# Packed wave tables, and the first weight tiles and gates brought forward, in a hybrid recurrence and Fourier block on one core

## The chip, the cores and the metric

The kernel runs on one core of one Trainium2 chip. Its metric is the device time of one execution in microseconds (us), of which several runs are given. TensorE is called PE here, VectorE DVE, ScalarE ACT, GpSimd POOL and SyncE SP; each works through its own instructions in order and waits on semaphores for the others.

## What is computed

A token block (2048 x 1024, float32) is normalised and projected by W_in. Half of the projection feeds a bidirectional gated recurrence with 8 heads, the other half a Fourier mix; both are gated and projected together by W_out, added to the input and normalised again. The parts that the change touches are the Fourier mix and the output product:

```python
def fourier_mix(u, w_four, b_four):
    ug = u.reshape(b_, length, FOURIER_GROUPS, FOURIER_GROUP_DIM)       # 4 groups of 256 channels
    spec = jnp.fft.fftn(ug, axes=(1, 3), norm="ortho").real
    y = jnp.einsum("blgc,gcd->blgd", spec, w_four).reshape(b_, length, FOURIER_WIDTH)
    return y + b_four
...
    y_a = o.reshape(h.shape[:-1] + (HGRN_WIDTH,)) * jax.nn.silu(gate_a)
    y_f = fourier_mix(u_f, w_four, b_four) * jax.nn.silu(gate_f)
    out = jnp.concatenate([y_a, y_f], axis=-1) @ w_out                  # W_out is 2048 x 1024
```

## The kernel before

Every float32 product is made of three passes over a high and a low part (`mm3`, L58 to L63): high by high, low by high, high by low. So each operand is split first: ACT copies it to the high part, DVE subtracts that from the raw values for the low part. All stages run in one program: `front` (norm, projections of the context, folded token sums), `heads` (projections and recurrence, up to about 1625 us of the trace) and `tail` (from there on), which the change touches.

`tail` has two halves. **The Fourier half** walks over four groups of 256 channels (`for n in range(FG)`). A group has, on PE: `middle(n)` (two small matmuls, L2673), `channels(n)` (eight steps f that fill the banks `ps_p`), then `waves(n, 0)` and `waves(n, 1)`, the transforms over time with the wave tables `tab_hi`, `tab_lo` for two blocks of 128 channels (m = 2n + c counts them), each with four arrays in the order 0, 2, 1, 3 and a few narrow matmuls at the end (L2724 to L2727, `ps_top`). ACT splits the high part of p (`split_p_high`), DVE the low part (`split_p_low`); PE may run only three steps of `channels` ahead of the low splits, since four banks hold p. After the transforms ACT copies the sine arrays out (`copy_sine`) and DVE joins them with the cosine arrays to y (`combine`, odd arrays by way of `mixed`); SP stores y to memory. DVE also folds the next group's input (`fold_again`, `split_fold_low`). All engines take these steps in an order written out by hand.

**The output half** multiplies the 16 row tiles of 128 tokens by W_out. W_out stands as 16 tiles of 128 x 1024 in on-chip memory, split too (`split_w_high` on ACT, `split_w_low` on DVE); tiles 8 to 15 belong to the Fourier rows, 0 to 7 to the heads. `W_ORDER` is the order of the splits, and j counts in it. A weight tile takes the place of something that is no longer read, so POOL waits before each load (`load_w`, L2045). PE starts with `f_part(0)`, `f_part(1)`, `f_part(2)` over six of eight Fourier tiles (`F_FIRST = 6`), which need the weights j = 0 to 5 and the gated, split rows `f_raw`, loaded from y in memory together with their gates `f_gate` (`load_f` on SP). Then come `turn_heads(0)` (transposes of the scaled head outputs), the remaining tiles, and `a_part`.

In the kernel before, all eight Fourier weight tiles are loaded and split in the last group (n = 3, `last`): the four wave tables take 64 KB, of which each 16 KB place holds only 4 KB of high and 4 KB of low part, and the folded input takes the rest.

## Time and profile before

| | |
|---|---|
| time, median of 3 runs (lowest to highest) | 2125.49 us (2124.35 to 2126.05) |
| the profiled execution | 2122.28 us |
| its span | 2120.3 us |
| mean granted clock of PE | 0.991 |
| PE busy | 2052.2 us (97%) |
| DVE busy | 1542.4 us (73%) |
| ACT busy | 537.6 us (25%) |
| chain that ended last | PE 88%, DVE 7%, issue, ACT, DMA and SP's queue 1% each |

The span runs from the first to the last instruction; the 2.0 us between it and the execution's time lie around it. "Busy" is a share of the whole span and tells little of one stage. The granted clock is a share of TensorE's full 2.4 GHz; 0.50 is 1.2 GHz. A row of a timeline gives start, duration, engine and line, the operation as out<-in, and in brackets the idle time before it and who ended it.

### The profile page before, as it was taken

Reading aid. Unit: us, or ns where it says so; the run is one execution under the profiler, and the core shown is the slowest. Engines: PE = TensorE matmul, PEld = TensorE weight load, DVE = VectorE, ACT = ScalarE, POOL = GpSimd, SP = SyncE. Lnnn points to the kernel's source line nnn. Section 1 sums busy time; section 2 is a strip of 40 time slices with the busy share of each in tenths; the row PEclk is TensorE's granted clock in tenths of the full one; section 3 lists DMA queues with packets and bytes.
Section 4 is the critical chain, followed back from the end, with each engine's and each line's share of the span. In section 5 each row is a group of like instructions: output and inputs, shape, how many; then the busy total and the mean of one; then the engine's idle time right before and its main releaser. Section 6 shows DMA issues by size and latency. Waiting matters only on the chain.

```text
span 2120.3 us, 51238 instructions
## 1 busy us (share of the span) xinstructions
PE 2052.2 (97%) x21168; PEld 1759.9 (83%) x21168; DVE 1542.4 (73%) x3318; ACT 537.6 (25%) x968; POOL 75.1 (4%) x109
## 2 busy tenths in 40 slices
PE   5899999999999999999999999999998989999997
PEld 2799998898888888888888888888887877888886
DVE  4865864143887878878887878799998986665664
ACT  3721134211122222212212221222213443222221
POOL 0001102000000000000000000000000010000000
PEclk9999999999999999999999999999999999999999
DMA  9534554323423324343333334243434377456461
GB/s 378 195 115 152 165 175 137 124 88 96 134 88 116 123 89 144 96 125 104 119 116 107 115 98 141 86 143 96 129 111 152 110 274 230 166 164 200 157 204 59
DMA packets 242542, 298.03 MB, mean 141 GB/s; under 512 B 15187, under 2 KB 172527, under 8 KB 240268
## 3 DMA queue, kind: packets, MB, share of 16 engines
q1 hardware_dynamic: 157868, 177.33, 26.5%
q10 hardware_dynamic: 74096, 81.18, 11.5%
q0 software_dynamic: 10352, 36.25, 5.4%
q8 instruction: 173, 2.83, 0.6%
q14 instruction: 53, 0.43, 0.1%
HBM read 197.11 MB, written 97.59 MB: 139 GB/s over the span
## 4 chain that ended last, share of the span: by engine, by line
PE 88%; DVE 7%; issue 1%; ACT 1%; DMA 1%; SPq 1%; ACTq 0%; DVEq 0%; POOL 0%
PE all_bank L61 19%; PE all_bank L63 19%; PE all_bank L62 19%; PE all_bank L1494 5%; PE all_bank L1500 5%; PE all_bank L1497 5%; PE all_bank L1572 3%; PE all_bank L1348 2%; PE all_bank L1528 2%; PE all_bank L1515 2%; PE all_bank L1565 1%; PE all_bank L71 1%; PE all_bank L1554 1%; PE all_bank L1347 1%; DVE hidden_h_lo L483 1%
## 5 line engine op out<-in xcount | busy, mean ns | idle before, releaser
L61 PE MATMUL all_bank<-hidden_h_hi,head_hi 128*128 128x512 f32 x718 | 288.1, 401 | 0.0
L63 PE MATMUL all_bank<-hidden_h_hi,head_lo 128*128 128x512 f32 x718 | 280.3, 390 | 0.0
L62 PE MATMUL all_bank<-hidden_h_lo,head_hi 128*128 128x512 f32 x718 | 279.9, 390 | 0.0
L1610 ACT ACTIVATE head_projected<-all_bank 128x512 f32<-128x512 f32 x148 | 88.6, 598 | 728.2 <-PE all_bank L63 460.9
L1494 PE MATMUL all_bank<-hidden_h_hi,head_hi 128*128 128x512 f32 x466 | 192.0, 412 | 0.6
L1708 DVE RECIPROCAL head_inverse<-head_gate 128x448 f32<-128x448 f32 x64 | 185.1, 2926 | 0.0
L1500 PE MATMUL all_bank<-hidden_h_hi,head_lo 128*128 128x512 f32 x466 | 182.2, 391 | 0.0
L1497 PE MATMUL all_bank<-hidden_h_lo,head_hi 128*128 128x512 f32 x466 | 181.9, 390 | 0.0
L63 PEld LDWEIGHTS all_bank<-hidden_h_hi,head_lo 128*128 128x128 f32 x718 | 134.8, 188 | 28.7
L61 PEld LDWEIGHTS all_bank<-hidden_h_hi,head_hi 128*128 128x128 f32 x718 | 134.9, 188 | 27.7
L62 PEld LDWEIGHTS all_bank<-hidden_h_lo,head_hi 128*128 128x128 f32 x718 | 135.1, 188 | 25.4
L61 PE MATMUL all_bank<-front_hi,hidden_h_hi 128*128 128x256 f32 x512 | 143.3, 280 | 0.0
L62 PE MATMUL all_bank<-front_lo,hidden_h_hi 128*128 128x256 f32 x512 | 142.3, 278 | 0.0
L63 PE MATMUL all_bank<-front_hi,hidden_h_lo 128*128 128x256 f32 x512 | 142.3, 278 | 0.0
L1375 DVE SCALAR_TENSOR_TENSOR head_state<-head_state,head_total,all_bank 128x128 f32<-128x128 f32 x256 | 71.8, 343 | 82.0 <-issue 65.3
L1748 DVE TENSOR_TENSOR head_query_planes<-head_query_planes,head_total 128x256 f32<-128x256 f32 x128 | 54.0, 422 | 71.9 <-PE all_bank L1515 35.4
L61 PE MATMUL all_bank<-tail_w_hi,tail_f_hi 128*128 128x512 f32 x256 | 101.0, 394 | 4.7 <-DVE tail_f_lo L2274 4.7
L1500 PEld LDWEIGHTS all_bank<-hidden_h_hi,head_lo 128*128 128x128 f32 x466 | 87.4, 188 | 19.4
L1494 PEld LDWEIGHTS all_bank<-hidden_h_hi,head_hi 128*128 128x128 f32 x466 | 87.5, 188 | 19.0 <-DVE head_lo L1652 1.9
L61 PE MATMUL all_bank<-tail_w_hi,tail_a_hi 128*128 128x512 f32 x256 | 101.5, 396 | 1.1 <-DVE tail_a_lo L2307 1.1
L62 PE MATMUL all_bank<-tail_w_lo,tail_f_hi 128*128 128x512 f32 x256 | 100.6, 393 | 0.0
L63 PE MATMUL all_bank<-tail_w_hi,tail_f_lo 128*128 128x512 f32 x256 | 100.5, 392 | 0.0
(327 smaller groups left out, 4778.3 us busy)
## 6 DMA issues: line engine op xcount, KB each, us to landing
head_raw<-in_w_in POOLq DMA_DIRECT2D x37, 512.0 KB, 5.0
head_value<-value_rows SPq DMA_DIRECT2D x64, 256.0 KB, 4.7
head_query<-piece_query SPq DMA_DIRECT2D x64, 256.0 KB, 5.6
head_out<-head_o ACTq DMA_DIRECT2D x64, 256.0 KB, 2.6
tail_o<-head_out SPq DMA_DIRECT2D x32, 512.0 KB, 6.5
front_raw<-in_w_in SPq DMA_DIRECT2D x19, 512.0 KB, 5.0
front_stage<-in_x SPq DMA_DIRECT2D x16, 512.0 KB, 6.6
front_w_mod<-in_w_ada SPq DMA_DIRECT2D x8, 1024.0 KB, 13.7
```

What stands on the lines that cost most here:

```text
L61: nc.tensor.matmul(out, st_hi, mv_hi, start=start, stop=False)
L62: nc.tensor.matmul(out, st_hi, mv_lo, start=False, stop=False)
L63: return nc.tensor.matmul(out, st_lo, mv_hi, start=False, stop=stop)
L1348: done = nc.tensor.matmul(ps[d][2][:, t, :], tile(query_far[d], t), state[d][:, before, :], start=g < NG // 2, stop=True)
L1375: nc.vector.scalar_tensor_tensor(state[d][:, j + 1, :], state[d][:, j, :], total_of(d, P)[:, j:j + 1], ps[d][1][:, t, :], ALU.mult, ALU.ad ...
L1494: nc.tensor.matmul(out, w_hi, tokens_hi, start=k == 0, stop=False)
L1497: nc.tensor.matmul(out, w_hi, tokens_lo, start=False, stop=False)
L1500: done = nc.tensor.matmul(out, w_lo, tokens_hi, start=False, stop=k == KT - 1)
L1572: done = nc.tensor.matmul(ps[d][1][:, t, :], key_t[d][:, t, :], value[d][b][:, t, :], start=True, stop=True)
L1610: nc.scalar.activation(projected[unit % 2][:], ps_proj[unit % 2][:], PIECES[name][1], scale=PIECES[name][2]).then_inc(proj_copied, 1)
L1708: nc.vector.reciprocal(in_blocks(inverse[d][:], d)[:, :, 1:BASE], in_blocks(gate[d][:], d)[:, :, 1:BASE]).then_inc(gated[d], 1)
L1748: nc.vector.tensor_tensor(qs, qs, tot[:, :, 0, :].to_broadcast(shape), ALU.mult)
```

## The change

The wave tables are packed into 32 KB. W_out's tiles 8 to 11 take the room that this frees: POOL loads them once the second group's input is split (`fold_lo_done` at 8), and their splits stand in the groups n = 1 (j = 0, 1) and n = 2 (j = 2, 3), ahead of the splits of p. In the last group j = 4, 5 stand at that place, j = 6, 7 at the place where j = 2, 3 stood, and two pairs of splits between and after the combines are gone. The other weight tiles shift along: the places in the folded input now hold 12 to 15, 0, 1, 4 and 5, and only 2, 3, 6 and 7 wait for the tables. The gates of row tiles 0, 1 and 2 are loaded whole in the group n = 1 with semaphores of their own (`f_gate_here`), and `load_f` issues only the rows for them. On ACT the high splits of `f_raw` 0 and 1 now stand ahead of `copy_sine(3, 1, 0)` instead of behind it.

```diff
-    tab_hi = [at(f"tab_hi{a}", [P, TIMES, QUART], TAB + 16 * KB * TAB_PLACE[a], F32R) for a in range(4)]
+    tab_hi = [at(f"tab_hi{a}", [P, TIMES, QUART], TAB + 8 * KB * TAB_PLACE[a], F32R) for a in range(4)]
...
+    W_FIRST, W_FOLD, W_TAB = range(KT, KT + 4), (12, 13, 14, 15, 0, 1, 4, 5), (2, 3, 6, 7)
+
     def w_slot(k):
-        return FOLD + HALF_LINE + (k - KT) * 8 * KB if k >= KT else TAB + (2 * TAB_PLACE[k // 2] + k % 2) * 8 * KB
+        if k in W_FIRST:
+            return TAB + (32 + 8 * (k - KT)) * KB
+        return FOLD + HALF_LINE + W_FOLD.index(k) * 8 * KB if k in W_FOLD else TAB + W_TAB.index(k) * 8 * KB
...
 (gpsimd)
+        for d in range(2):
+            pool.wait_ge(left.o_copied[d], left.steps)
+        pool.wait_ge(fold_lo_done, 8)
+        for k in W_FIRST:
+            load_w(k)
         pool.wait_ge(fold_lo_done, 4 * FG)
-        load_w(KT)
-        load_w(KT + 1)
+        for k in W_FOLD[:2]:
+            load_w(k)
         pool.wait_ge(mid_done, FG)
-        load_w(KT + 2)
-        load_w(KT + 3)
+        for k in W_FOLD[2:4]:
+            load_w(k)
         pool.wait_ge(p_done, 8 * FG)
-        for k in range(KT + 4, 2 * KT):
+        for k in W_FOLD[4:]:
             load_w(k)
         for a in A_ORDER:
             pool.wait_ge(y_done, y_turn(M_LAST, a))
-            load_w(2 * a)
-            load_w(2 * a + 1)
+            load_w(W_TAB[TAB_PLACE[a]])
...
 (sync, in the loop over groups)
                 load_w(n + 1)
+                if n == 1:
+                    for sem in left.proj_stored:
+                        sp.wait_ge(sem, left.all_units // 2 * DMA)
+                    for t in range(3):
+                        load_f_gate(t)
...
 (vector, in the loop over groups; scalar likewise with split_w_high)
             split_middle_low(n)
-            if last:
-                split_w_low(0)
-                split_w_low(1)
+            if n:
+                split_w_low(2 * n - 2)
+                split_w_low(2 * n - 1)
             for f in range(8):
                 split_p_low(n, f)
...
             else:
-                split_w_low(2)
-                split_w_low(3)
+                split_w_low(6)
+                split_w_low(7)
             v.wait_ge(small_here, len(small) * DMA)
             combine(n, 0, 0)
-            if last:
-                split_w_low(4)
-                split_w_low(5)
             combine(n, 0, 1)
...
             else:
-                split_w_low(6)
-                split_w_low(7)
                 gate_f_part(0)
                 gate_f_part(1)
             combine(n, 1, 0)
...
 (scalar, last group)
             else:
-                split_w_high(6)
-                split_w_high(7)
-            copy_sine(n, 1, 0)
-            if last:
                 split_f_high(0)
                 split_f_high(1)
+            copy_sine(n, 1, 0)
             copy_sine(n, 1, 1)
```

DVE at the start of the second group (n = 1), where `tail_mid_lo` is the low part of the middle row, `tail_p_lo` the low parts of p and `tail_w_lo` those of W_out. Before:

```order
L2222 TENSOR_TENSOR tail_mid_lo<-all_bank,tail_mid_hi 1x256
L2227 TENSOR_TENSOR tail_p_lo_26309<-all_bank,tail_p_hi_26305 128x512 x2
L2227 TENSOR_TENSOR tail_p_lo_26310<-all_bank,tail_p_hi_26306 128x512 x2
L2227 TENSOR_TENSOR tail_p_lo_26311<-all_bank,tail_p_hi_26307 128x512 x2
L2227 TENSOR_TENSOR tail_p_lo_26312<-all_bank,tail_p_hi_26308 128x512 x2
```

After, at the same place:

```order
L2242 TENSOR_TENSOR tail_mid_lo<-all_bank,tail_mid_hi 1x256
L2279 TENSOR_TENSOR tail_w_lo_26366<-tail_w_raw_26350,tail_w_hi_26334 128x1024
L2279 TENSOR_TENSOR tail_w_lo_26367<-tail_w_raw_26351,tail_w_hi_26335 128x1024
L2247 TENSOR_TENSOR tail_p_lo_26309<-all_bank,tail_p_hi_26305 128x512 x2
L2247 TENSOR_TENSOR tail_p_lo_26310<-all_bank,tail_p_hi_26306 128x512 x2
L2247 TENSOR_TENSOR tail_p_lo_26311<-all_bank,tail_p_hi_26307 128x512 x2
L2247 TENSOR_TENSOR tail_p_lo_26312<-all_bank,tail_p_hi_26308 128x512 x2
```

Two weight splits stand ahead of the eight splits of p; the third group has the same with j = 2, 3, and the last group had it already and keeps it.

DVE in the last group, from the first combine of m = 6 to the gating of the first rows (`tail_f_raw`). Before:

```order
L2252 SCALAR_TENSOR_TENSOR tail_y_26314<-all_bank,tail_b_cols,tail_sine 128x255
L2259 TENSOR_TENSOR tail_w_lo_26370<-tail_w_raw_26354,tail_w_hi_26338 128x1024
L2259 TENSOR_TENSOR tail_w_lo_26371<-tail_w_raw_26355,tail_w_hi_26339 128x1024
L2239 TENSOR_TENSOR tail_mixed<-all_bank,tail_sine 128x512
L2240 TENSOR_TENSOR tail_mixed<-all_bank,tail_sine 128x512
L2243 SCALAR_TENSOR_TENSOR tail_y_26314<-tail_mixed,tail_b_cols 128x256
L2244 SCALAR_TENSOR_TENSOR tail_y_26314<-tail_mixed,tail_b_cols 128x256
L2245 SCALAR_TENSOR_TENSOR tail_y_26314<-tail_mixed,tail_b_cols 128x256
L2246 SCALAR_TENSOR_TENSOR tail_y_26314<-tail_mixed,tail_b_cols 128x256
L2259 TENSOR_TENSOR tail_w_lo_26372<-tail_w_raw_26356,tail_w_hi_26340 128x1024
L2259 TENSOR_TENSOR tail_w_lo_26373<-tail_w_raw_26357,tail_w_hi_26341 128x1024
L2268 TENSOR_TENSOR tail_f_raw_26377<-tail_f_raw_26377,tail_f_gate_26383 128x768
```

After:

```order
L2272 SCALAR_TENSOR_TENSOR tail_y_26314<-all_bank,tail_b_cols,tail_sine 128x255
L2259 TENSOR_TENSOR tail_mixed<-all_bank,tail_sine 128x512
L2260 TENSOR_TENSOR tail_mixed<-all_bank,tail_sine 128x512
L2263 SCALAR_TENSOR_TENSOR tail_y_26314<-tail_mixed,tail_b_cols 128x256
L2264 SCALAR_TENSOR_TENSOR tail_y_26314<-tail_mixed,tail_b_cols 128x256
L2265 SCALAR_TENSOR_TENSOR tail_y_26314<-tail_mixed,tail_b_cols 128x256
L2266 SCALAR_TENSOR_TENSOR tail_y_26314<-tail_mixed,tail_b_cols 128x256
L2289 TENSOR_TENSOR tail_f_raw_26377<-tail_f_raw_26377,tail_f_gate_26383 128x768
```

Both pairs of weight splits have left this stretch.

## Rows read from the trace of the kernel before

**Rows 1.** Timeline of PE, starts of the transforms (L2717) of three groups.
```profile
1668.98 0.37 PE L2717 MATMUL all_bank<-tail_sign_row,tail_mid_hi 1*128 1x256 f32 x1
...
1694.02 0.37 PE L2717 MATMUL all_bank<-tail_sign_row,tail_mid_hi 1*128 1x256 f32 x1
...
1716.87 0.36 PE L61 MATMUL all_bank<-tail_cw_hi,tail_fold_hi 128*128 128x256 f32 x1 [1.30 <-DVE tail_p_lo L2227]
...
1720.58 0.37 PE L2717 MATMUL all_bank<-tail_sign_row,tail_mid_hi 1*128 1x256 f32 x1
```

**Rows 2.** Timeline of DVE, starts of the groups n = 1 and n = 3.
```profile
1655.31 2.49 DVE L2206 TENSOR_TENSOR tail_fold_lo<-tail_fold,tail_fold_hi 128x512 fp32r<-128x512 f32 x4
...
1663.78 0.41 DVE L2222 TENSOR_TENSOR tail_mid_lo<-all_bank,tail_mid_hi 1x256 fp32r<-1x256 f32 x1
...
1713.44 0.41 DVE L2222 TENSOR_TENSOR tail_mid_lo<-all_bank,tail_mid_hi 1x256 fp32r<-1x256 f32 x1
```

**Rows 3.** DMA issues around 1707.4 (median us to landing), and POOL's line L2045.
```profile
tail_w_raw<-in_w_out POOLq DMA_DIRECT2D x2, 512.0 KB, 5.3
...
DMA to landing us min/median/max: 4.1/8.1/12.0
```

**Rows 4.** Timeline of PE, ends of blocks m = 5, 6, 7, then the output half.
```profile
1709.70 0.17 PE L2724 MATMUL all_bank<-tail_sign_cols,tail_p_hi 128*128 128x2 f32 x1
...
1726.13 0.17 PE L2724 MATMUL all_bank<-tail_sign_cols,tail_p_hi 128*128 128x2 f32 x1
...
1731.21 0.36 PE L61 MATMUL all_bank<-tail_tab_hi,tail_p_hi 128*128 128x256 f32 x1 [0.60 <-DVE tail_mixed L2240]
...
1734.72 0.24 PE L2727 MATMUL all_bank<-tail_sign_row,tail_mid_lo 1*128 1x2 f32 x1
...
1739.66 0.80 PE L61 MATMUL all_bank<-tail_w_hi,tail_f_hi 128*128 128x512 f32 x1 [4.70 <-DVE tail_f_lo L2274]
...
1780.50 1.09 PE L2772 MATMUL all_bank<-all_ident,tail_o 128*128 128x128 f32 x8 [1.49 <-DVE tail_o L2293]
```

**Rows 5.** Stretches: us, busy PE, PEld, DVE, ACT, POOL (x), PEclk, DMA share, GB/s.
```profile
13.30:13.80 0.50, 0.00 (x0) 0.00 (x0) 0.21 (x1) 0.48 (x2) 0.00 (x0) 1.00 1.00 410
...
58.00:59.00 1.00, 0.48 (x1) 0.18 (x1) 1.00 (x3) 0.97 (x4) 0.00 (x0) 0.56 0.99 387
...
1737.50:1738.00 0.50, 0.00 (x0) 0.00 (x0) 0.50 (x2) 0.50 (x2) 0.00 (x0) 0.50 0.97 410
...
1744.00:1744.50 0.50, 0.50 (x3) 0.36 (x2) 0.50 (x1) 0.00 (x0) 0.00 (x0) 0.70 1.00 410
```

**Rows 6.** Timeline of PE in the front stage, two waits.
```profile
14.74 1.94 PE L1058 MATMUL all_bank<-front_w_mod,front_silu_wide 128*32 128x512 f32 x8 [2.98 <-DMA front_w_mod<-in_w_ada]
...
58.50 0.48 PE L924 MATMUL all_bank<-all_ident,front_stage 128*128 128x128 f32 x1 [1.74 <-DVE front_stage L475]
```

**Rows 7.** Timeline of DVE, an undisturbed odd combine, then the end of the last group.
```profile
1710.53 0.69 DVE L2239 TENSOR_TENSOR tail_mixed<-all_bank,tail_sine 128x512 f32<-128x512 f32 x1 [0.71 <-ACT tail_sine L2497]
...
1734.96 1.82 DVE L2268 TENSOR_TENSOR tail_f_raw<-tail_f_raw,tail_f_gate 128x768 f32<-128x768 f32 x2
1736.69 1.14 DVE L2249 SCALAR_TENSOR_TENSOR tail_y<-all_bank,tail_b_cols,tail_sine 128x512 f32<-128x512 f32 x1
...
1738.66 1.81 DVE L2274 TENSOR_TENSOR tail_f_lo<-tail_f_raw,tail_f_hi 128x768 fp32r<-128x768 f32 x2
...
1752.20 0.96 DVE L2268 TENSOR_TENSOR tail_f_raw<-tail_f_raw,tail_f_gate 128x768 f32<-128x768 f32 x1 [7.63 <-DMA tail_f_gate<-piece_gate_f]
```

**Rows 8.** Timeline of ACT, end of the last group.
```profile
1735.94 1.71 ACT L2517 ACTIVATE tail_f_hi<-tail_f_raw 128x768 fp32r<-128x768 f32 x2 [2.37 <-DVE tail_f_raw L2268]
1737.56 0.58 ACT L2497 ACTIVATE tail_sine<-all_bank 128x512 f32<-128x512 f32 x1
```

**Rows 9.** DMA issue of the second row tile around 1721.3 (us to landing).
```profile
tail_f_raw<-fourier_out SPq DMA_DIRECT2D x1, 384.0 KB, 10.8
```

**Rows 10.** Line L2866 on POOL, the last block: count, ns, first and last start.
```profile
L2866 POOLq EVENT_SEMAPHORE_RANGE_CLEAR  x52: 44/44/44, 2116.0 to 2119.9; - x52
```

More of the change, by code:

```diff
@@ L2034, in f_landed, with gate_landed @@
         t = F_SPLITS[n][0]
-        return sum(f_set(s) == f_set(t) for s, _, _ in F_SPLITS[:n + 1]) * 2 * DMA
+        return sum(f_set(s) == f_set(t) for s, _, _ in F_SPLITS[:n + 1]) * DMA
+    def gate_landed(n):
+        t = F_SPLITS[n][0]
+        return (1 + sum(s >= 3 and f_set(s) == f_set(t) for s, _, _ in F_SPLITS[:n + 1])) * DMA
     @block.gpsimd
@@ L2086, in load_f @@
             s = f_set(t)
-            for dst, src in ((f_raw[s], y_f), (f_gate[s], gate_f)):
-                sp.dma_start(dst[:, first:end, :], src[first * P:end * P, t * P:(t + 1) * P].rearrange("(k p) t -> p k t", p=P)
-                             ).then_inc(f_here[s], DMA)
+            sp.dma_start(f_raw[s][:, first:end, :], y_f[first * P:end * P, t * P:(t + 1) * P].rearrange("(k p) t -> p k t", p=P)
+                         ).then_inc(f_here[s], DMA)
+            if t >= 3:
+                load_f_gate(t)
         def load_o(t):
@@ L2128, in _ @@
                 load_w(n + 1)
+                if n == 1:
+                    for sem in left.proj_stored:
+                        sp.wait_ge(sem, left.all_units // 2 * DMA)
+                    for t in range(3):
+                        load_f_gate(t)
             else:
                 sp.wait_ge(p_done, 8 * FG)
[L2131 to L2132 removed]
                 for c in range(CC):
```

25 lines of the change are left out of this document (12 added, 13 removed).

## The prediction

> **What bounds the kernel now.** First the busy shares and the chain that ended last: PE carries 97% of the span and 88% of the chain, so a change pays only where PE stands still or runs slow. Next the waits of PE and its timeline in the tail. Between the last transform and the output product PE is idle for 4.70 us and is released by DVE's low split of the first rows; shortly before, it waits 0.60 us for `mixed` [rows 4]. The stretches by clock show a second price: at 1737.5, with PE idle since 1734.96, the granted clock is 0.50 (1.2 GHz), and it is back at full speed only inside the slice 1744.00 to 1744.50, whose mean is 0.70 [rows 5]. A slice of 0.5 us with mean 0.70 is 0.3 us at half and 0.2 us at full speed, so the clock rose at 1744.3. PE started at 1739.66, hence 4.64 us of matmuls ran at half speed and cost 2.3 us. Last I read who is late at 1739.66: DVE goes from the second row gate straight to a combine and the low split [rows 7], so DVE's queue in the last group is what ends last there.
>
> Third, PE waits 1.30 us in `channels(3)` for the low splits of p, the place where the last group already has two weight splits ahead of them [rows 1]. The groups before show no such wait. The change builds this very order into the groups n = 1 and 2.
>
> **The costs, step by step.** I count on the time axis of the trace of before and sum the shifts.
>
> Group n = 2: the starts of the transforms lie at 1668.98, 1694.02 and 1720.58 [rows 1]. The second distance is 26.56 us, the first 25.04, both with the same work on PE; the two weight splits cost 1.5 us (the wait of 1.30 and its restart). DVE reaches the low middle split at the same point of the group in both, so n = 2 will pay the same **1.5 us**. That DVE makes up for the delay later in the group does not give it back, for PE has no other wait there.
>
> Group n = 1: DVE is later against PE. In the last group the transforms (1720.58) start 7.14 us after the middle split (1713.44); in n = 1 that split stands at 1663.78 [rows 2], which gives 1670.92 where it was 1668.98: 1.9 us. It holds if the weights are there. `fold_lo` is done at 1657.8 [rows 2], POOL's four loads follow at about 1658.1, 1658.7, 1659.2 and 1659.7. In the last group a pair of such loads landed 5.3 us after issue in the median [rows 3], also behind a store of y. The first lands at about 1663.2, the second at 1664.3. ACT needs about 1.1 us and DVE 1.2 us for each, so the second low split ends near 1666.7 instead of 1666.4. With that, **2.1 us**. Ends: 1.5 (as n = 2) and 3.4, if the second lands 1.3 us later because four queue instead of two.
> The Trainium skill, "DMA: Bandwidth & Descriptors", section "Anatomy of one DMA", gives about 2.0 us plus bytes over 436 GB/s for a load of this path, 3.2 us for one such tile. By that both tiles would be in time and this term 1.9; the trace shows 5.3, with other traffic beside it, and I keep the row.
>
> The wait of 0.60 us: DVE's splits j = 4, 5 are gone from between the combines. In m = 5 `mixed` starts at 1710.53, 0.83 us after the narrow matmuls at 1709.70 [rows 4, 7]. In m = 6 those stand at 1726.13, so `mixed` starts at 1726.96 and is done more than 2 us before PE wants it at 1730.61: **-0.6 us**. PE ends the transforms at 1734.36 instead of 1734.96.
>
> The wait of 4.70 us: an odd combine takes 2.91 us (from 1710.53 to the next operation, 1713.44) [rows 2, 7]. From 1726.96 it ends at 1729.87. The gating follows at once if the rows are there: the first tile needs 0.98 us until ACT starts its high split (1734.96 to 1735.94), so that starts at 1730.85. ACT's two high splits now stand ahead of the sine copy, which comes 1.62 us later [rows 8], at 1732.47; it takes 0.58 us, DVE's combine of m = 7 begins at 1733.1. That combine lasts 1.97 us (1736.69 to 1738.66) and the first low split releases PE 1.00 us after its start [rows 4, 7]: 1736.07. PE is ready at 1734.36, so 1.7 us of the 4.7 remain: **-3.0 us**. What is late next is this combine behind ACT, no longer DVE's queue. The second row tile must land by 1730.8. It took 10.8 us behind a gate load [rows 9]; issued at 1720.6 it would at worst be there at 1731.4 and cost 0.6. Without the gate load ahead of it I take it as in time.
>
> The clock: a gap of 2.98 us in the front stage left it at 1.00 [rows 5, 6], so one of 1.7 should leave it there too: **-2.3 us**.
>
> After that the gain must survive. The third row tile cannot be loaded until the last combine, now 3.4 us earlier. DVE waited 7.63 us, to 1752.20, for its gate [rows 7], which is now long there, so its part moves by about 5 us or more. PE's demand moves by 0.6 + 3.0 + 2.3 = 5.9. The stage absorbs the rest: PE waits 1.49 us at 1780.50 [rows 4] for a load that its own first block releases, which moves with PE, and up to 1.5 us of lateness ahead of it is swallowed there. Loads of `f_raw` 6 and later keep their gates, so nothing changes from there on.
>
> Small parts: three semaphores more are cleared at the end, 52 took 3.9 us [rows 10], **+0.2 us**. SP's three gate loads (1.5 MB) stand behind the loads that the second group needs and ahead of a store that waits for DVE much longer; the projection stores they wait for were waited for by ACT a group earlier. Cost nothing while DMA has room there; if not, they push the same store, whose data is read only in the last group. POOL's new wait has only POOL's own loads behind it. Packing the tables changes no operation.
>
> Sum: 2.1 + 1.5 - 0.6 - 3.0 - 2.3 + 0.2 = **-2.1 us** on the profiled execution's 2122.28 us. The median of the runs lies 3.2 us above that execution; I put the same difference on the median: 2125.5 - 2.1 = **2123.4 us**, 0.1% less.
>
> **Rivals.** (a) The clock falls again at the shorter gap. For it: 58.00 to 59.00 shows 0.56 after a wait of only 1.74 us [rows 5, 6], with little work ahead of it, and here the gap follows narrow matmuls too. Against: 2.98 us without a fall. The price is at most the old 2.3 us: 2125.7.
> The Trainium skill, "TensorE: Matmul & The Clock Gate", part 1, says that the monitor runs free of the program, so where it switches varies from run to run; the two rows above point the same way, and my chance for (a) comes from them.
> (b) The early weights land late and become the bound, which ends slower. Price: each us beyond 1664.3 for the second tile adds one us to n = 1. From 2.1 us late the whole change is a loss. The slowest weight load took 12.0 us [rows 3]: landing at 1670.7, 6.4 us late, plus a clock fall of 2.3: 2123.4 + 8.7 = 2132.1. Against: those 12.0 were behind eight loads and two stores; here one store of y is nearly done.
> (c) The gap closes wholly and the groups cost less: 1.7 more gained, and 1.3 in each group (the bare wait) instead of 3.6 in all. 2123.4 - 1.7 - 1.0 = 2120.7. For it: DVE idles about 1 us per group that it can make up. Against: the order on ACT fixes the combine.
> (d) The change does not do what it says, if the stage is bound by PE's stalls in all groups alike: gains and costs cancel, 2125.5.
>
> **How the numbers follow.** My forecast 0.58, (a) 0.15, (b) 0.07, (c) 0.12, (d) 0.08. About 0.2%, 4.25 us, is what a measurement of this kernel can tell from no change. The forecast, (a) and (d) lie within it; of (b) about two thirds end beyond it; (c) reaches it (2121.2) with most of its chance, and of the forecast a little. That gives faster 0.15, within 0.80, slower 0.05. The range takes (c) and (a), and the end 3.4 of n = 1 with 0.6 for the late row tile on top of (a), which would be 2127.6 together; one of them is the likelier: 2120.7 to 2127.0.
>
> **What would show it.** In the trace of the changed kernel: a distance of 26.5 us instead of 25.04 between the starts of the transforms of n = 1 and n = 2, and 26.5 again to n = 3; waits of PE for `tail_p_lo` of about 1.8 us in `channels(1)` and 1.3 in `channels(2)`; no wait for `tail_mixed` in m = 7; a wait of 1.7 us instead of 4.7 before the first `tail_w_hi`, still released by `tail_f_lo`; a clock of 1.00 through it. A wait of ACT for `tail_w_raw` above 3 us in n = 1 would mean (b); a clock of 0.50 after the gap (a). The prediction is wrong if DVE's lag grows from group to group, which would add to each group more than 1.5 us, or if the third row tile or the first transposes make PE wait for more than the 1.5 us that the stage swallows.

## The result and the profile after

The changed kernel takes **2126.98 us** (median of 21 runs, 2124.21 to 2128.29); the kernel before took 2123.51 us beside it (21 runs, 2120.15 to 2127.24). The ratio is 1.0016, 95% interval 1.0009 to 1.0022: 0.16% or 3.5 us slower, where 0.1% faster was predicted. Each experiment below was run with executions of the kernel before in the same series, and its ratio is to those; two single executions of 5044.97 and 6824.42 us, in the second series of e10, are left out of the ratios. The profiled execution took 2126.24 us, its span 2124.4 us (before 2122.28 and 2120.3), both at a mean clock of 0.991.

First PE's own timeline of the kernel after, from the waves of m = 1 on. A row gives start, duration, engine and line, operation, and the idle time ahead with who ended it. L2727 is the line that was L2717, L2736 was L2726, L2782 was L2772.

```profile
1653.02 0.37 PE L2727 MATMUL all_bank<-tail_sign_row,tail_mid_hi 1*128 1x256 f32 x1
...
1660.49 0.27 PE L2736 MATMUL all_bank<-tail_sign_row,tail_mid_hi 1*128 1x2 f32 x1
...
1667.22 0.36 PE L61 MATMUL all_bank<-tail_cw_hi,tail_fold_hi 128*128 128x256 f32 x1 [1.30 <-DVE tail_p_lo L2247]
1670.92 0.37 PE L2727 MATMUL all_bank<-tail_sign_row,tail_mid_hi 1*128 1x256 f32 x1
...
1693.77 0.36 PE L61 MATMUL all_bank<-tail_cw_hi,tail_fold_hi 128*128 128x256 f32 x1 [1.30 <-DVE tail_p_lo L2247]
1697.48 0.37 PE L2727 MATMUL all_bank<-tail_sign_row,tail_mid_hi 1*128 1x256 f32 x1
...
1724.03 0.37 PE L2727 MATMUL all_bank<-tail_sign_row,tail_mid_hi 1*128 1x256 f32 x1
...
1737.34 0.24 PE L2737 MATMUL all_bank<-tail_sign_row,tail_mid_lo 1*128 1x2 f32 x1
1740.29 0.80 PE L61 MATMUL all_bank<-tail_w_hi,tail_f_hi 128*128 128x512 f32 x1 [2.70 <-DVE tail_f_lo L2295]
1768.08 1.03 PE L2782 MATMUL all_bank<-all_ident,tail_o 128*128 128x128 f32 x8
...
1797.88 1.03 PE L2782 MATMUL all_bank<-all_ident,tail_o 128*128 128x128 f32 x8
1820.79 1.03 PE L2782 MATMUL all_bank<-all_ident,tail_o 128*128 128x128 f32 x8
```

Read against [rows 1] and [rows 4]: the distance to n = 2 is 26.56 us instead of 25.04, as predicted; the wait for `mixed` is gone; the gap of 4.70 us is 2.70. The last two rows show what no row above has: two head turns (the eight transposes of one row tile) of the steady output half stand 22.91 us apart.

Next DVE and then ACT ahead of the output half, in the kernel after:

```profile
1733.32 0.95 DVE L2289 TENSOR_TENSOR tail_f_raw<-tail_f_raw,tail_f_gate 128x768 f32<-128x768 f32 x1
1734.97 0.96 DVE L2289 TENSOR_TENSOR tail_f_raw<-tail_f_raw,tail_f_gate 128x768 f32<-128x768 f32 x1 [0.70 <-DMA tail_f_raw<-fourier_out]
...
1737.33 1.14 DVE L2269 SCALAR_TENSOR_TENSOR tail_y<-all_bank,tail_b_cols,tail_sine 128x512 f32<-128x512 f32 x1 [1.40 <-ACT tail_sine L2513]
...
1739.29 1.81 DVE L2295 TENSOR_TENSOR tail_f_lo<-tail_f_raw,tail_f_hi 128x768 fp32r<-128x768 f32 x2
```
```profile
1734.31 0.85 ACT L2533 ACTIVATE tail_f_hi<-tail_f_raw 128x768 fp32r<-128x768 f32 x1 [3.62 <-DVE tail_f_raw L2289]
1735.96 0.84 ACT L2533 ACTIVATE tail_f_hi<-tail_f_raw 128x768 fp32r<-128x768 f32 x1 [0.81 <-DVE tail_f_raw L2289]
1736.72 1.07 ACT L2513 ACTIVATE tail_sine<-all_bank 128x512 f32<-128x512 f32 x2
```

DVE waits 0.70 us for the second row tile's transfer, ACT's `f_hi` waits for DVE, the copy of the sine stands behind `f_hi`, and the combine waits 1.40 us for the sine. The clock behind the gap (stretch, PE's busy time, granted clock, DMA share, GB/s):

```profile
1738.00:1739.00 1.00, 0.00 (x0) 1.00 1.05 442
1739.00:1740.00 1.00, 0.00 (x0) 0.71 0.91 377
1740.00:1742.00 2.00, 1.71 (x4) 0.50 1.00 373
1742.00:1744.00 2.00, 2.00 (x6) 0.50 0.64 262
1744.00:1746.00 2.00, 2.00 (x6) 0.50 0.65 270
1746.00:1747.00 1.00, 1.00 (x5) 0.88 1.06 295
```

The clock fell inside the gap of 2.70 us (a mean of 0.71 is full speed up to 1739.4) and stayed at half speed into the last slice (a mean of 0.88 is a quarter of it at half), to 1746.2, so 5.9 us of matmuls cost 3.0 us.

Last, twelve row tiles of the output half, before and then after, from one head turn to the twelfth behind it. PE is busy throughout, the clock is 1.00, and the numbers of matmuls are equal:

```profile
1819.20:2091.76 272.56, 272.56 (x1249) 1.00 0.54 173
```
```profile
1820.79:2095.66 274.87, 274.87 (x1249) 1.00 0.53 171
```

The same work takes 22.71 us a row tile before and 22.91 after, without a wait. The sum of the differences between the two traces from `channels` on, each as the difference of a distance in after and in before: `channels(0)`, in which the clock was 0.50 for some 3 us in after only, and the waves of m = 0 +0.6, the waves of m = 1 +1.5, from there to the transforms of n = 1 +1.0, n = 2 +1.5, the last group -0.8, the gap -2.0, from the first output matmul to the second head turn +0.7, from there to the last head turn +2.6 (313.88 instead of 311.26 us), the end +0.2: +5.3 us; the tail started 1.2 us earlier, which leaves the 4.1 us between the spans.

### The profile page after: what moved, and what is told of

The parts are those of the page before. It is cut to its first block, busy times and chain, and to the rows that moved or that the text cites. A ratio compares the mean times of both kernels' runs of the same rounds, so it can differ in the third digit from the quotient of the medians.

```text
span 2124.4 us, 51258 instructions
## 1 busy us (share of the span) xinstructions
PE 2055.9 (97%) x21168; PEld 1761.8 (83%) x21168; DVE 1541.6 (73%) x3318; ACT 537.4 (25%) x968; POOL 74.8 (4%) x109
## 4 chain that ended last, share of the span: by engine, by line
PE 87%; DVE 7%; DMA 2%; issue 1%; ACT 1%; SPq 1%; ACTq 0%; DVEq 0%
PE all_bank L61 20%; PE all_bank L63 19%; PE all_bank L62 19%; PE all_bank L1494 5%; PE all_bank L1500 5%; PE all_bank L1497 5%; PE all_bank L1572 3%; PE all_bank L1528 2%; PE all_bank L1348 2%; PE all_bank L1515 2%; PE all_bank L1565 1%; PE all_bank L71 1%; PE all_bank L1554 1%; DVE hidden_h_lo L483 1%; PE all_bank L1347 1%
## 5 line engine op out<-in xcount | busy, mean ns | idle before, releaser
L63 PE MATMUL all_bank<-tail_w_hi,tail_a_lo 128*128 128x512 f32 x256 | 100.7, 393 | 0.0
```

The source lines that it names most:

```text
L63: return nc.tensor.matmul(out, st_lo, mv_hi, start=False, stop=stop)
```

## The experiments

In the output half the row tile (f or a, high or low part) stands in the array, the stationary operand, and the weight tile streams past it, the moving one. Where a group of six matmuls is named below, it is the time from the first matmul of one weight tile to that of the next (two column halves, three products each), a mean over 11 or 12 row tiles from 1820 us on. An offset is a tile's start inside 8 KB of the tail's room; `HALF_LINE` is 64 bytes, a tile of W_out 8 KB.

### Is it the place of the weight tiles?

**e1**, the kernel before with

```diff
-        return FOLD + HALF_LINE + (k - KT) * 8 * KB if k >= KT else ...
+        return FOLD + (k - KT) * 8 * KB if k >= KT else ...
```

> The kernel before with one change: W_out tiles 8 to 15 stand 64 bytes lower, so that they begin in the other half of a 128-byte line than the row tiles f_hi and f_lo with which TensorE multiplies them. Same instructions, same order, same waits. Theory H (halves): in the kernel after, W 8 to 11 stand in another half than f, and their groups of six matmuls took 1.373 to 1.375 us from start to start where before had 1.360; so with all eight tiles apart the groups of W 9 to 15 go from 1.360 to about 1.373, the distance between two head turns from 22.71 to about 22.80 us, and the whole kernel gets about 1.5 us slower. Rival R (company): the slower groups come from what other engines and transfers do beside them, and the place of a weight tile is without effect: 22.71 us, no change of the total.

Measured 2126.98 us, 1.0017 (1.0007 to 1.0027) of before. All eight groups of W 8 to 15 take 1.400 us (before 1.360, the first 1.373), so the effect is three times what was expected; the distance of head turns is 23.03 us. R falls. The starts of the groups of W 9 and W 15, six groups apart, in the kernel before and in e1:

```profile
1826.90 0.39 PE L61 MATMUL all_bank<-tail_w_hi,tail_f_hi 128*128 128x512 f32 x1
...
1835.07 0.39 PE L61 MATMUL all_bank<-tail_w_hi,tail_f_hi 128*128 128x512 f32 x1
```
```profile
1827.71 0.40 PE L61 MATMUL all_bank<-tail_w_hi,tail_f_hi 128*128 128x512 f32 x1
...
1836.11 0.40 PE L61 MATMUL all_bank<-tail_w_hi,tail_f_hi 128*128 128x512 f32 x1
```

That is 8.17 and 8.40 us for the same 36 matmuls. The lines of PE's groups over twelve row tiles, busy time and mean ns of one matmul, of the kernel before and of e1:

```profile
L61 PE MATMUL all_bank<-tail_w_hi,tail_f_hi 128*128 128x512 f32 x192 | 74.7, 389 | 0.0
```
```profile
L61 PE MATMUL all_bank<-tail_w_hi,tail_f_hi 128*128 128x512 f32 x192 | 76.0, 396 | 0.0
...
L61 PE MATMUL all_bank<-tail_w_hi,tail_a_hi 128*128 128x512 f32 x192 | 75.8, 395 | 0.0
```

Only the product whose weight tiles were moved has changed (a had 396 before). The 7 ns more for each matmul are the 0.04 us of a group.

**e2**, likewise for tiles 0 to 7 (`TAB - HALF_LINE + ...`):

> The kernel before with one change: W_out tiles 0 to 7 stand 64 bytes lower, so that they begin in the other half of a 128-byte line than the row tiles a_hi and a_lo. Same instructions, order and waits. Theory H (halves): in the kernel after, W 0, 1, 4 and 5 stand in another half than a, and their groups took 1.400 us where before had 1.382, 1.382 and 1.360; with all eight apart the distance between head turns goes from 22.71 to between 22.8 and 22.95 us and the kernel gets 1.5 to 4 us slower. Rival R (company): 22.71 us, no change. If this run or its sister for tiles 8 to 15 shows nothing and the other does, the half matters only for that product.

2125.86 us, 1.0015 (1.0006 to 1.0024). The groups of W 0 to 7 take 1.400 us (1.490 with the head turn in it), those of f stay at 1.360. 22.99 us a row tile. Again the place, and again only of the product that was moved.

**e3**, the kernel after with

```diff
-        return FOLD + HALF_LINE + W_FOLD.index(k) * 8 * KB if k in W_FOLD else ...
+        return FOLD + W_FOLD.index(k) * 8 * KB if k in W_FOLD else ...
-    F_SETS = (SMALL_W, SMALL_W + 8 * KB, ROWS)
+    F_SETS = (SMALL_W - HALF_LINE, SMALL_W + 8 * KB - HALF_LINE, ROWS - HALF_LINE)
```

> The kernel after with all weight tiles and all row tiles (f and a) in the same half of a 128-byte line: the eight weight tiles in the first 64 KB and the three f sets stand 64 bytes lower. Everything else as in the kernel after: the same tiles in the same regions, instructions, order and waits. Theory H (halves): the distance between head turns goes back from 22.91 to about 22.71 us and the kernel is about 3 us faster than the kernel after, near the kernel before. Rival R (company) and rival D (the distance or the region in which a weight tile stands, not its half): 22.91 us stays, and the total stays 3 to 4 us above the kernel before.

2130.35 us, 1.0026 (1.0017 to 1.0036): not faster. The trace shows 22.99 us a row tile instead of 22.91. W 8 to 11 went from 1.373 to 1.397 us, W 0, 1 and 4 stayed at 1.394 to 1.399, W 13 to 15 and W 2, 3, 6 and 7 take 1.36. My theory of halves falls: these tiles shared the half of the line. What the slow ones have in common is that row tile and weight tile differ by 128 bytes; those at 1.36 have the same offset. Theory O, that the difference of offsets counts, was formed here.

**e8**, the kernel after with every tile at the same offset, 128 bytes:

```diff
-        return FOLD + HALF_LINE + W_FOLD.index(k) * 8 * KB if k in W_FOLD else ...
+        return FOLD + 2 * HALF_LINE + W_FOLD.index(k) * 8 * KB if k in W_FOLD else ...
-    F_SETS = (SMALL_W, SMALL_W + 8 * KB, ROWS)
+    F_SETS = (SMALL_W + HALF_LINE, SMALL_W + 8 * KB + HALF_LINE, ROWS - HALF_LINE)
```

> The kernel after with every weight tile and every row tile (f and a) at the same offset inside 8 KB (the eight weight tiles in the first 64 KB and the two f sets stand 64 bytes higher, the third f set 64 lower). Theory H (halves of 128 bytes) has fallen with the run that put all tiles in the same half: its groups for W 8 to 11 went up to 1.397 us and W 0, 1, 4 stayed at 1.398, though they shared the half and differed from the row tile by 128 bytes. Theory O (offset): what counts is the difference of the two tiles' offsets; at 0 a group of six matmuls takes 1.360 us, at 64 or 128 up to 1.400. Under O every group of the row tiles here takes 1.36 us (but for the one behind the head turn), the distance of two head turns is 22.71 us, and the kernel is 2.6 to 3.2 us faster than the kernel after. Rival D (the distance or the region in which a tile stands): W 8 to 11 and W 0, 1, 4, 5 stay slow, 22.9 us.

2124.37 us, 1.0007 (0.9998 to 1.0016). By the ratios (1.0016 for the kernel after) that is about 2 us less than the kernel after; their intervals overlap, so the proof is the trace. Twelve row tiles in e8:

```profile
1822.06:2093.98 271.92, 271.92 (x1250) 1.00 0.56 173
```

22.66 us a row tile, less than the kernel before: every group but the one with the head turn takes 1.360 us. The kernel before had the products of its steady stream at equal offsets, but a and f at two different ones (128 and 64 bytes), and the groups behind a change from one product to the other (W 8; W 0 and 1) took 1.373 to 1.382 us. Rival D falls, for no tile changed its region.

**e9**, the kernel before with differences in steps:

```diff
-        return FOLD + HALF_LINE + (k - KT) * 8 * KB if k >= KT else ...
+        return FOLD + (k - KT) * 8 * KB + (k - KT) // 2 * 32 if k >= KT else ...
-    F_SETS = (SMALL_W, SMALL_W + 8 * KB, ROWS)
+    F_SETS = (SMALL_W + HALF_LINE, SMALL_W + 8 * KB + HALF_LINE, ROWS)
-    A_PLACE = (PARTS + 24 * KB, F_SETS[1])
+    A_PLACE = (PARTS + 24 * KB + 4 * HALF_LINE, F_SETS[1])
```

> The kernel before with differences of offset in steps: the f sets stand 64 bytes higher, W 8 and 9 stand 128 bytes below the offset of f, W 10 and 11 96, W 12 and 13 64, W 14 and 15 32 bytes; the a tiles stand 256 bytes above the offset of W 0 to 7. Theory O in the form that any difference costs the same: all eight groups of W 8 to 15 take 1.400 us, and those of W 0 to 7 too. In the form that the cost grows with the difference: 1.400, 1.400 and less for 64 and 32. In the form of a pattern that repeats: W 0 to 7 at 256 bytes stay at 1.360 us. It tells which differences a planner of places has to avoid; the total says little here.

2127.55 us, 1.0022 (1.0013 to 1.0031). All runs together, by the row tile's offset minus the weight tile's:

| difference, bytes | group of six matmuls, us | where |
|---|---|---|
| 0 | 1.360 | all in e8; before |
| 32 | 1.39, 1.40 | W 14, 15 in e9 |
| 64 | 1.40 | e1, e2; W 0, 1, 4 of after; 1.39, 1.40 in e9 |
| 96 | 1.403, 1.407 | W 10, 11 in e9 |
| 128 | 1.39 to 1.40 | W 8, 9 in e9; W 0, 1, 4 in e3 |
| 256 | 1.360 | W 0 to 7 in e9 |
| -64 | 1.373 | W 8 to 11 of after |
| -128 | 1.397 | W 8 to 11 in e3 |

The step from 0 to 32 bytes costs nearly all, more distance costs no more, and at 256 the cost is gone. That is a pattern that repeats. The table counts the starts of whole tiles, but a matmul takes one slice of the row tile (`f_hi[s][:, k, :]`, 512 bytes a step) and one column half of the weight tile (2 KB a step), so the slices at difference 0 stand multiples of 512 bytes apart, and those of W 0 to 7 in e9 256 bytes more. All of them take 1.360 us, so every multiple of 256 bytes that occurs here is free. If only the difference inside 256 bytes counts, -128 is the same as 128, and they agree (1.397 and 1.39 to 1.40), and -64 is 192, the only point between 128 and 256; why it costs a third of 64 stays open.

### Is it the place of the early splits?

**e6**, the kernel after with the splits of two weight tiles in each group behind the splits of p (on ACT likewise):

```diff
             split_middle_low(n)
-            if n:
-                split_w_low(2 * n - 2)
-                split_w_low(2 * n - 1)
             for f in range(8):
                 split_p_low(n, f)
...
                     fold_again(n + 1, a)
-            else:
+            if n:
+                split_w_low(2 * n - 2)
+                split_w_low(2 * n - 1)
+            if last:
                 split_w_low(6)
                 split_w_low(7)
```

> The kernel after with the splits of two weight tiles in each of groups 1, 2 and 3 moved on ScalarE and VectorE from ahead of the p splits to behind them (VectorE: behind the folding of the next group; ScalarE: ahead of the first copy of the sines). All else as in the kernel after. Theory P (place): the splits cost time only because TensorE's transforms wait for p_lo at the head of a group; behind p they lie in time that VectorE has to spare, the distances between the starts of two groups' transforms go from 26.56 us to about 25.0 (what group 2 of the kernel before took, without any split there) for groups 2 and 3, and from 29.4 to some 27 for group 1, 4 to 5 us in all. Rival L (load): VectorE is the bound over a whole group, so the splits cost the same wherever they stand: 26.5 us stays. A gain in between means that VectorE has less spare time than the two splits need (1.1 to 1.3 us a group).

2123.46 us, 0.9998 (0.9989 to 1.0007): by the ratios (0.9998 against 1.0016) 3.8 us of the loss are back, with the output half still at 22.9 us a row tile. PE in e6:

```profile
1670.25 0.37 PE L2727 MATMUL all_bank<-tail_sign_row,tail_mid_hi 1*128 1x256 f32 x1
...
1679.85 0.35 PE L61 MATMUL all_bank<-tail_tab_hi,tail_p_hi 128*128 128x256 f32 x1 [0.28 <-DVE tail_y L2272]
...
1696.12 0.37 PE L2727 MATMUL all_bank<-tail_sign_row,tail_mid_hi 1*128 1x256 f32 x1
...
1721.97 0.37 PE L2727 MATMUL all_bank<-tail_sign_row,tail_mid_hi 1*128 1x256 f32 x1
...
1729.74 0.36 PE L61 MATMUL all_bank<-tail_tab_hi,tail_p_hi 128*128 128x256 f32 x1 [1.41 <-DVE tail_y L2272]
```

The distances are 25.87 and 25.85 us instead of 26.56: no wait for `p_lo`, but one of 0.28 for the combine, and in the last group, with four splits in a row, one of 1.41. The place is worth 0.7 of the 1.5 us a group; 0.8 us a group remain, so the load on DVE is not free there either, and the result is neither P's 25.0 nor L's 26.5. From the end of the waves of m = 1 to the second head turn e6 takes 118.19 us where after takes 121.29: 2.4 us less up to the transforms of n = 3, 1.5 more in them for the wait of 1.41, and 2.2 less behind them, where the gap is 1.53 us instead of 2.70.

### What held the gap at 2.70 us?

**e4**, the kernel after with the sine's copy ahead of the f splits on ACT, as in the kernel before:

```diff
+            copy_sine(n, 1, 0)
             if last:
                 split_f_high(0)
                 split_f_high(1)
-            copy_sine(n, 1, 0)
```

> The kernel after with one change on ScalarE in the last group: the copy of the first sine of m = 7 stands ahead of the two splits of f again, as in the kernel before. Theory S: in the kernel after VectorE's combine of m = 7 waited 1.40 us for this copy, which stood behind f_hi(0) and f_hi(1), and these behind the transfer of f_raw(1); with the copy ahead the gap before the first tail_w_hi matmul shrinks from 2.70 to about 1.3 us, and the kernel is 1 to 1.5 us faster than the kernel after (more, up to 4, if the clock of 0.50 behind the gap goes too). Rival T (the transfer): the first matmul of the output half needs f_lo of both parts anyway, and f_raw(1) lands where it does: 2.7 us stays, within 0.3.

```profile
1737.12 0.51 PE L61 MATMUL all_bank<-tail_w_hi,tail_f_hi 128*128 128x512 f32 x1 [0.47 <-DVE tail_f_lo L2295]
```

The gap is 0.47 us, less than S expected, and the clock stays at 1.00 behind it: 25.05 us to the first head turn instead of 27.79. Measured 2124.1 us, 1.0012 (1.0003 to 1.0021); from the transforms of n = 0 to the third head turn its profile is 4.9 us shorter than that of after, but the ratios (1.0012 and 1.0016) do not tell the two kernels apart. Not all of the 2.23 us is the sine's place: in e4 DVE did not wait for the second row tile. e3 has the sine behind f, as after has, and no such wait either:

```profile
1739.02 0.79 PE L61 MATMUL all_bank<-tail_w_hi,tail_f_hi 128*128 128x512 f32 x1 [1.92 <-DVE tail_f_lo L2295]
```

So the sine's place is worth 1.92 - 0.47 = 1.45 us, about what S gave, and the late transfer is worth the other 0.78. T names a second cause and not the only one.

**e5**, the kernel after with W 0, 1, 4 and 5 loaded behind the sines of m = 6:

```diff
-        pool.wait_ge(p_done, 8 * FG)
+        pool.wait_ge(y_done, y_turn(M_LAST - 1, A_ORDER[-1]))
         for k in W_FOLD[4:]:
```

> The kernel after with one change on GpSimd's queue: W 0, 1, 4 and 5 are loaded when the sines of m = 6 are done, 7 us later, and no longer beside f_raw(0) and f_raw(1). Theory C (contention): f_raw(1) took 10.6 us to land because these four transfers of 512 KB each stood in the engines with it; without them it lands within 6 to 8 us, VectorE's wait of 0.70 us for tail_f_raw and with it part of the gap of 2.70 us goes: 1.7 to 2.0 us. Rival Q: the transfer of f_raw is slow by itself (10.8 us beside the gate's in the kernel before), and the gap stays at 2.7 us. The four weights are needed 25 us later; if they come late the wait stands in front of the first a part of the output half.

The DMA view of the stretch 1715 to 1740 in after, then in e5 (issues, KB each, median us from issue to landing), and e5's first output matmul:

```profile
tail_f_raw<-fourier_out SPq DMA_DIRECT2D x2, 384.0 KB, 8.0
```
```profile
tail_f_raw<-fourier_out SPq DMA_DIRECT2D x2, 384.0 KB, 3.6
```
```profile
1739.86 0.80 PE L61 MATMUL all_bank<-tail_w_hi,tail_f_hi 128*128 128x512 f32 x1 [1.92 <-DVE tail_f_lo L2295]
```

The four weight transfers, issued from 1723.69 in after, 0.15 us ahead of the first of the two of `f_raw`, doubled the latter's time; without them the wait for the transfer is gone and the gap is 1.92 us. The clock still fell (26.49 us to the head turn). Theory C holds for the transfer: it took 3.6 to 4.0 us in the four profiles with the weights loaded later (e5, e10, e18, e19) and 6.0 to 10.1 in the others that come from after. But the gap of 1.92 us alone does not show it, since e3 has the same gap with the four loads in place. There they were issued 0.20 us behind `f_raw`:

```profile
tail_f_raw<-fourier_out SPq DMA_DIRECT2D x2, 384.0 KB, 6.4
```

Issued 0.2 to 0.3 us ahead of the weights (e3, e4) `f_raw` takes 6.4 and 6.0 us and is in time; 0.15 to 0.4 us behind the first of them (after, e8, and the second series of after, e14) it takes 8.0 to 8.2 and DVE waits 0.70 to 1.08 us. Measured 2124.89 us, 1.0014 (1.0005 to 1.0023), too small a step for the measurement to show.

### The repairs together, and the change without its side effects

**e10** joins e8, e6, e4 and e5; **e12** the first three.

> The kernel after with four repairs at once: all weight and row tiles at equal offsets inside 8 KB; the early weight splits behind the p splits; the first sine of m = 7 copied ahead of the f splits; W 0, 1, 4 and 5 loaded 7 us later. If the four act on separate places, the terms add up from their own profiles: 3.7 us (distance of two head turns 22.91 to 22.66), 2.5 + 0.7 + 0.7 us (groups 1, 2, 3 at 26.85, 25.87, 25.85 us), the gap before the output half at 0.5 us or less instead of 2.70 with the clock's fall gone (about 5 us from the last wave to the head turn of row tile 1): some 11 to 12 us faster than the kernel after, 2115 to 2117 us, about 8 below the kernel before. Rival B (back-up): VectorE, which now reaches the splits 4 and 5 later, hands f_lo over later, and the gap stays at 1.5 us as in the run with the splits moved: 2 to 3 us less gain.

> As the run with four repairs, but the four weight tiles are loaded as early as in the kernel after. If the contention of these transfers with f_raw matters once the copy of the sine stands ahead, this kernel has the larger gap before the output half, by up to 0.8 us; if f_raw lands in time for what is left of the gap, both are the same within 0.3 us in the profile (the measurement can't tell less than 2 us).

e10: **2116.97 us, 0.9977 (0.9965 to 0.9988)**, faster than both kernels, 9.8 us below the kernel after, which took 2126.76 us in the same series (e14). The end of its last group:

```profile
1732.50 1.81 DVE L2295 TENSOR_TENSOR tail_f_lo<-tail_f_raw,tail_f_hi 128x768 fp32r<-128x768 f32 x2
```

`f_lo` starts at 1732.50 while PE is still in the waves of m = 7, so no wait is left there; 22.66 us a row tile. B, a back-up, does not show. e12: 2117.65 us, 0.9981 (0.9972 to 0.9990), the same within the measurement. In its profile `f_raw` took 10.1 us to land, and DVE, which has four splits ahead of it there, still did not wait for it. A second series of e10 (2119.36 us beside 2124.24, e18 below) gave 0.9972 (0.9957 to 0.9987).

**e13**, the kernel before with equal offsets and the splits of W 8 and 9 behind p:

> The kernel before, without packed tables and without early weights, with two of the repairs: equal offsets for W 8 to 15 and the f sets with the other tiles, and the splits of W 8 and 9 behind the p splits in group 3. It tells what the change itself is worth once its side effects are out. Expected from the rows: the distance of two head turns from 22.71 to 22.66 us (0.7 us in all), group 3 from 26.56 to 25.8 us; the gap of 4.70 us before the output half and the clock's fall behind it stay, since all eight splits still stand there: 2121 to 2122 us. Then the change's own worth is the difference to the run with three repairs, 5 to 6 us. Rival: the splits moved behind p lengthen the gap by what they saved in front, and the total stays at the kernel before.

2121.35 us, 0.9999 (0.9991 to 1.0008). The row tile takes 22.66 us and the group before n = 3 25.04. The gap of 4.70 us did not stay, as was expected: it is 1.66 us. But four splits in a row ahead of the combine make PE wait 1.44 us before the waves of m = 7, and in this profile these ran at half clock for a part (8.84 us instead of about 5.98), so that, as the rival has it in kind, what was saved came back elsewhere. e12, which has the same two repairs and the sine first, as the kernel before has it, shows what the early weights are worth once their side effects are out: 2117.65 against 2121.35 us, 3.7 us by the medians and 3.8 by the ratios, less than the 5 to 6 expected; with the later weight loads (e10) it is about 4.5.

### The waves of m = 1: changed kernel or chance?

In after, e3, e4, e5, e8 and e12 these waves took 7.47 to 7.49 us from sign row to sign row, with the clock at 0.50 for some 3 us; in before, e1, e2, e6, e9, e10 and e13 5.98 us. Up to there nothing in the work differs but places. The clock in these waves, of the kernel before and of its second execution (e15, below):

```profile
1655.00:1658.00 3.00, 3.00 (x27) 1.00 0.63 262
```
```profile
1655.00:1658.00 3.00, 3.00 (x16) 0.50 0.53 218
```

> The kernel after once more, unchanged. In five of the five profiled kernels that have the splits of W 8 and 9 ahead of the p splits of group 1, the granted clock fell to 0.50 some 2.4 us after the wait of 1.2 us before the waves of m = 1, and the time from one sign row matmul to the next there was 7.47 us; in five of five others it stayed at 1.00 and the time was 5.98 us, though nothing differs up to that place. If it is the luck of a phase, this run may show 5.98 us; if it belongs to the kernel, it shows 7.47 us, and the two runs with splits behind p in this batch show 5.98. The total: 2126 to 2127 us.

> The kernel before, unchanged, profiled once more. If the clock's fall in the waves of m = 1 is the luck of a phase, it shows here with a chance of about one half (7.47 us from sign row to sign row); if it belongs to the kernel after, never: 5.98 us.

> The kernel before a third time, with the same question: luck gives 7.47 us in about half of the executions, a cause in the changed kernel gives 5.98 us always.

> The kernel with the early splits behind the p splits once more. Its first profile showed 5.98 us in the waves of m = 1. Luck: about half a chance of 7.47 us now. A cause that lies in the program: 5.98 us again.

> The kernel with four repairs once more: 5.98 us in the waves of m = 1 if that belongs to the program, 7.47 with a chance of one half if it is luck. The total: again 0.997 to 0.999 of the kernel before.

The kernel after showed 7.48 us again (2126.76 us, 1.0023, 1.0014 to 1.0033). But so did both further executions of the kernel before, and e6 and e10 on their second profile, 7.47 each. The kernel before, second execution:

```profile
1653.94 0.37 PE L2717 MATMUL all_bank<-tail_sign_row,tail_mid_hi 1*128 1x256 f32 x1
...
1661.41 0.27 PE L2726 MATMUL all_bank<-tail_sign_row,tail_mid_hi 1*128 1x2 f32 x1
...
1670.31 0.37 PE L2717 MATMUL all_bank<-tail_sign_row,tail_mid_hi 1*128 1x256 f32 x1
```

So the same program has it in one execution and not in the next: it is not fixed by the change, and the +1.5 us between the two profiles is not counted as its cost. Whether all kernels fall equally often is not shown: it was 2 of 7 profiles of kernels in before's order, 4 of 6 with the early splits behind p, and 6 of 6 with them ahead of p. These rows also mend the account of n = 1. With the slow waves the kernel before needs 8.90 us from the last sign row to the transforms (9.41 without), since DVE has more time to come up; the kernel after, which had them in both its profiles, needs 10.43. Like with like, n = 1 costs **1.53 us**, the same as n = 2. With fast waves the same order was never profiled. The Trainium skill says in "TensorE: Matmul & The Clock Gate", part 1 ("What's actually happening"), that the monitor runs free of the kernel; by that the same wait meets it differently from run to run, and these traces agree: a wait of about 1.2 us was followed by the fall in some executions of one program and not in others.

### One step further

**e19**, e10 with the splits of W 14 and 15 behind the last combine instead of ahead of the first of the last group, on both engines.

> The kernel with four repairs, with the splits of W 14 and 15 moved behind everything that stands ahead of the output half on ScalarE and VectorE. Theory W: the wait of 1.41 us before the waves of m = 7 is VectorE's four splits of 1.16 us each ahead of the first combine; with two of them gone it vanishes, and with it the place at which the clock fell: m = 7 then takes 5.98 us in every execution, 1.4 us of wait and (in the executions that had it) 2.4 us of slow clock less: 1.4 to 3.8 us faster than the run with four repairs, 2113 to 2116 us. Rival: W 14 and 15 are needed 8 and 9.5 us behind the first matmul of the output half, and their splits stand there behind combine and ahead of the splits with gate of the a weights; if they are late, TensorE waits there instead, and the head turns come as late as now.

2115.28 us, **0.9963 (0.9949 to 0.9977)**, the fastest kernel here. PE in e19:

```profile
1727.65 0.37 PE L2725 MATMUL all_bank<-tail_sign_row,tail_mid_hi 1*128 1x256 f32 x1
...
1733.63 0.27 PE L2734 MATMUL all_bank<-tail_sign_row,tail_mid_hi 1*128 1x2 f32 x1
...
1734.47 0.50 PE L61 MATMUL all_bank<-tail_w_hi,tail_f_hi 128*128 128x512 f32 x1 [0.46 <-DVE tail_f_lo L2295]
...
1768.80 0.50 PE L61 MATMUL all_bank<-tail_w_hi,tail_a_hi 128*128 128x512 f32 x1 [2.76 <-DVE tail_a_lo L2328]
```

The wait of 1.41 us at m = 7 is gone and the waves run at full clock (5.98 us; with the wait, e18 had 8.36 and e10 5.98, so one profile does not show that the fall is gone in every execution). But DVE's two splits push its later work, and PE now waits 2.76 us for `a_lo` (e10: 1.42), and the clock falls to 0.50 behind it for some 3 us, which it did not in e10: from the first output matmul to the second head turn e19 takes 41.52 us, e10 38.68. The rival was right that a wait comes back, wrong in which: W 14 and 15 were in time. The intervals of e10 and e19 overlap, so that e19 is the better is likely and not shown.

## Why the prediction was wrong

Two steps failed, and neither alone would have made this loss out of the gain.

- **"Packing the tables changes no operation", "nothing changes from there on": a term put at nothing.** The packing put W 8 to 11 at an offset 64 bytes above f's and W 0, 1, 4 and 5 at one 64 below a's. Each group of the former takes 1.373 instead of 1.360 us, of the latter 1.400 instead of 1.36 to 1.38: 0.2 us a row tile, **+2.6 us** from the second head turn to the last. e1, e2, e3 and e8 show it from four sides. I took equal instructions as equal time.
- **The clock, -2.3 us: wrong in sign against the kernel before.** It fell again, and cost 3.0 instead of 2.3 us, **+0.7** where -2.3 stood. This is rival (a), which I gave 0.15, though my rows had one wait of 2.98 us without a fall and one of 1.74 us with one [rows 5, 6]. Behind gaps of 1.92 us it fell too (e3, e5), behind 0.47 us it did not (e4). The executions of m = 1 show the same wait of 1.2 us with and without a fall, so one row without a fall bears no certainty.
- **The gap, -3.0 us**, measured -2.0: a size. The chain of causes was right (DVE's combine behind ACT's sine behind `f_hi`), and e4 confirms it; where the second row tile was in time, the gap was 1.92 us (e3) against the 1.7 predicted. The rest is that tile, of which I said "I take it as in time": it was 0.70 us late although no gate load stood ahead, beside POOL's four weight loads (e5).
- **n = 2, +1.5 us**: right, 1.52. **n = 1, +2.1 us**: 1.53 like with like. The lag that I carried over from the last group was right: from the middle split (1663.80) to the transforms (1670.92) the kernel after needs 7.12 us where I had 7.14, and ACT did not wait for a weight, so the 0.2 us for late weights and rival (b) fall. The difference is that slow waves make the kernel before later too. **The wait for `mixed`, -0.6**: right (-0.8 with what follows), though in other executions of the kernel before that wait was 0.67 us (e15) or under 0.25 (e16). **The end, +0.2**: right.
- The time that the stage ahead of the turns should swallow was swallowed: PE waited 1.60 us at 1781.78 where it had waited 1.49.

With the corrected terms (1.5, 1.5, -0.8, -2.0, +0.7 from the first output matmul to the second turn, +2.6, +0.2) the sum is +3.7 us; measured +3.5. Against the predicted -2.1 the clock makes 3.0 us of the difference, the offsets 2.6 and the gap 1.0; n = 1 and the waves take 0.8 back.

That 2126.98 us lies just inside the stated 2120.7 to 2127.0 is luck: the forecast stood on a median of three runs, 2125.49, and 21 runs of the same kernel gave 2123.51.

## What to carry to other kernels

When a change moves tiles, compare not only the instructions but the start of each stationary tile with that of the moving tile it meets, and keep the two at equal offsets, or a multiple of 256 bytes apart; here 32 to 128 bytes apart cost 2 to 3.5% of a steady stream of matmuls in which nothing waits and the clock is full. A slower steady stream is seen only by the distance between two marks over many rounds, for no view lists it as idle time. And work that is taken out of a gap and put ahead of what the next engine waits for can cost there what it gave here (3.0 us in two groups, for 2.0 in the gap): put it behind that, which is cheaper though not free, and keep other queues' transfers from starting just ahead of the one that ends the gap.

## What the runs showed of the hardware

The cost of offsets was not expected: 1.360 us for six matmuls of 512 columns at a difference of 0 or 256 bytes, 1.39 to 1.407 at 32 to 128, 1.397 at -128, 1.373 at -64. The Trainium skill says in "TensorE: Matmul & The Clock Gate", part 2 ("Step-by-step: what each phase is for"), that loading the next tile's weights "doesn't steal SBUF read bandwidth from the running matmul". Here the weight loads are the row tiles, and a shift of one operand against the other by 64 bytes alone slowed every matmul by 7 ns (e1); the runs show that the two streams are not independent of each other's addresses, though not where they meet. The other surprise is how short a wait precedes a fall of the clock: 1.19 to 1.22 us, in 12 of 19 profiled executions of kernels that do the same work up to there. The clock fell 1.7 to 2.1 us after the wait had ended (not 2.4, as the expectation of e14 says), with PE busy again. Each fall cost 1.5 us in the waves of m = 1, of which the kernel before got 0.5 back by n = 1.
